# A fused attention, state-space and feed-forward layer: clamped decays, rows of the second weight pair loaded into spent space, and two steps in another order

## The reference

```
h    = rms_norm(x, pre_mix_w) * (1 + scale1) + shift1
q, k, v, xs, z, bm, cm, dt = split(h @ w_in)
attn = sliding window attention over blocks of 128 tokens (8 heads of 64)
ssm  = mamba2_mixer(xs, z, bm, cm, dt)           # 8 heads of 64, state 128, 2 groups
x    = x + gate1 * rms_norm(concat(attn, ssm) @ w_out, post_mix_w)
h    = rms_norm(x, pre_ffn_w) * (1 + scale2) + shift2
u    = causal_dwconv3(h @ w_up)                  # 1024 x 5632
x    = x + gate2 * rms_norm((gelu(u_gate) * u_val) @ w_down, post_ffn_w)
```

```
decay  = exp(segsum(dt * a))                     # zero above the diagonal
y_diag = einsum(cb * decay, xc)                  # cb = C B^T inside a block
y      = (y_diag + y_off + d_skip * xh) * silu(z)
y      = rms_norm over each of 2 groups of 256, times norm_w
```

## Time and profile before

| | |
|---|---|
| median of 3 runs | 1139.71 us (1139.21 to 1140.12) |
| the profiled execution | 1136.96 us, span 1135.0 us |
| TensorE busy | 1080.2 us, 95% of the span |
| VectorE busy | 867.8 us, 76% |
| ScalarE busy | 560.8 us, 49% |
| GpSimd busy | 250.1 us, 22% |
| largest groups of TensorE | L2099 407.1 us, L2496 359.5 us, L2429 393.5 us in its last stretch |
| chain that ended last | PE 80%, DVE 9%, ACT 4%, DMA 3%, issue 2% |

### The profile page before, as it was taken

The page is one execution under the profiler, slowest core; times in us unless marked ns, Lnnn a source line. Parts: engine busy times, 40 slices in busy tenths (PEclk is TensorE's granted clock), DMA queues, the critical chain, the costliest instruction groups (busy, mean ns, idle before and its releaser), DMA issues.

```text
span 1135.0 us, 14878 instructions
## 1 busy us (share of the span) xinstructions
PE 1080.2 (95%) x5096; PEld 868.2 (77%) x5096; DVE 867.8 (76%) x1121; ACT 560.8 (49%) x1012; POOL 250.1 (22%) x237
## 2 busy tenths in 40 slices
PE   4699999999989999997999999999999999999997
PEld 4578766766767888765888888888888888888885
DVE  5869676767558688778888888888888877777687
ACT  4812254556464655665544444444444545454453
POOL 2000011111224442215333333333333100000012
PEclk9899999999999999998999999999999999999999
DMA  9989401001234222224343434343433595632324
GB/s 355 307 265 319 131 23 34 20 20 37 58 113 146 76 94 74 74 73 150 132 163 112 153 124 153 124 145 132 145 132 111 193 388 206 213 102 93 102 85 167
DMA packets 117487, 157.40 MB, mean 139 GB/s; under 512 B 15292, under 2 KB 76221, under 8 KB 117437
## 3 DMA queue, kind: packets, MB, share of 16 engines
q1 hardware_dynamic: 117117, 155.69, 40.9%
q0 software_dynamic: 320, 1.06, 0.3%
HBM read 125.75 MB, written 30.98 MB: 138 GB/s over the span
## 4 chain that ended last, share of the span: by engine, by line
PE 80%; DVE 9%; ACT 4%; DMA 3%; issue 2%; POOL 1%; SPq 1%; DVEq 0%; POOLq 0%; ACTq 0%
PE ps L2429 35%; PE ps L2099 18%; PE ps L2496 18%; DVE big L1387 3%; DMA raw<-in_w_in_dram 2%; PE ps L2138 2%; PE ps L2164 1%; PE ps L2152 1%; DMA scratch<-in_rel_bias_dram 1%; DVE big L1765 1%; DVE w_lo L1428 1%; PE ps L2269 1%; PE ps L2055 1%; PE ps L2368 1%; PE ps L2197 1%
## 5 line engine op out<-in xcount | busy, mean ns | idle before, releaser
L2099 PE MATMUL ps<-a_hi,w_hi 128*128 128x512 f32 x416 | 142.7, 422 | 7.5 <-DVE a_lo L1447 3.8
L2099 PE MATMUL ps<-a_lo,w_hi 128*128 128x512 f32 x416 | 132.6, 397 | 0.0
L2099 PE MATMUL ps<-a_hi,w_lo 128*128 128x512 f32 x416 | 131.8, 395 | 0.0
L2496 PE MATMUL ps<-w_hi,a_hi 128*128 128x512 f32 x308 | 119.9, 389 | 0.2 <-DVE a_lo L1931 0.2
L2496 PE MATMUL ps<-w_lo,a_hi 128*128 128x512 f32 x308 | 119.8, 389 | 0.0
L2496 PE MATMUL ps<-w_hi,a_lo 128*128 128x512 f32 x308 | 119.8, 389 | 0.0
L1299 ACT ACTIVATE w_hi<-raw 128x512 fp32r<-128x512 f32 x77 | 48.7, 632 | 98.3 <-PE ps L2496 87.6
L2099 PEld LDWEIGHTS ps<-a_hi,w_hi 128*128 128x128 f32 x416 | 73.3, 192 | 29.6 <-issue 16.3
L1219 ACT ACTIVATE scratch<-ps 128x512 f32<-128x512 f32 x88 | 52.3, 594 | 87.0 <-PE ps L2429 87.0
L2099 PEld LDWEIGHTS ps<-a_hi,w_lo 128*128 128x128 f32 x416 | 79.2, 190 | 18.2
L2099 PEld LDWEIGHTS ps<-a_lo,w_hi 128*128 128x128 f32 x416 | 79.5, 191 | 17.8
(11 more groups left out here) (267 smaller groups left out, 2394.0 us busy)
## 6 DMA issues: line engine op xcount, KB each, us to landing
big<-in_w_ada_dram SPq DMA_DIRECT2D x20, 1024.0 KB, 8.7
raw<-in_w_up_dram SPq DMA_DIRECT2D x22, 512.0 KB, 5.1
big<-in_w_up_dram SPq DMA_DIRECT2D x22, 512.0 KB, 5.1
big<-in_w_down_dram SPq DMA_DIRECT2D x22, 512.0 KB, 6.4
down_weight_sums<-big SPq DMA_DIRECT2D x22, 512.0 KB, 3.4
raw<-down_weight_sums SPq DMA_DIRECT2D x44, 256.0 KB, 2.8
ffn_hidden<-big SPq DMA_DIRECT2D x21, 512.0 KB, 2.6
big<-ffn_hidden SPq DMA_DIRECT2D x21, 512.0 KB, 8.4
```

What stands on the lines that cost most here:

```text
L2099: mm = pe.matmul(out, lhs_of[a], rhs_of(b, j), start=first and p == 0, stop=last and p == 2)
L2496: mm = pe.matmul(bk, a[:, ts], rhs_op(s)[w], start=fresh and m == 0, stop=last and m == 2, skip_group_check=s // KH in (J6, J3, J7))
```

## The change

1. **Decays.** The sums are kept with their sign (`sums`, before `neg_sums`). ScalarE no longer waits for GpSimd but for the loaded row. For each group it does four Relu of 128x128, relu(sum - row), waits for them, and then one Exp of 128x512 with scale -1. For allowed pairs that is the same value as before; for the future it is at most 1, whatever the sum. VectorE makes `cbm`, C B with the future set to zero (128x256, out of PSUM, times the triangle `upper`), waits for it, and multiplies the decays by `cbm` in place of the PSUM bank. `no_future` and GpSimd's `decay_mask` are gone.
2. **Pair 1's rows.** At the last block SyncE waits until pair 0's first low part is made, pair 0's sums are made, the last scaling by norm_w is done and the a1 rows have landed. Then it loads a21 and, below, a11 and a12 of pair 1 into `raw_pair(0)`, and a22 into `normw`. The load behind the token sums is gone. GpSimd's sums of pair 1 read there and no longer wait for pair 0's sums to be split; pair 2's load waits for them (`s_us` at 4).
3. **Order.** In the last unit `z_transpose` stands a step ahead of `state_product`. ScalarE squares the gated rows of block 0 ahead of the third `w_out_hi`.
4. **Copy of pair 1.** ScalarE copies product 0 of pair 1 ahead of the high part of s34 and of pair 0's Gelu.

Context lines and renamed semaphores are left out of the diff.

```diff
--- before.py
+++ after.py
@@ -199,9 +199,9 @@
         bn = scratch[:, 3328:3584].rearrange("p (g n) -> p g n", g=2)
-        no_future = scratch[:, 3072:3200]
+        cbm = scratch[:, 3072:3328].rearrange("p (g n) -> p g n", g=2)
         sum_rows = scratch[0:NB * H, 3200:3328]
-        neg_sums = scratch[:, 3584:3648]
+        sums = scratch[:, 3584:3648]
@@ -316,8 +316,8 @@
-            if isinstance(p, int) and p == 1 and kind == "a1":
-                return scratch[:, 2048:3072]
+            if isinstance(p, int) and p == 1 and kind in ("a1", "a22"):
+                return scratch[:, 2048:3072] if kind == "a1" else normw[:, :]
             return {"a1": raw_pair(par)[:, 0:1024], "s12": weight_sum(p)[0], "a22": raw_pair(par)[:, 1536:2048],
@@ -615,6 +615,19 @@
                     load_decay(b + 3)
+                if b == NB - 1:
+                    sp.wait_ge(s_ul, weights_to(0, "a1"))
+                    sp.wait_ge(s_us, 2)
+                    sp.wait_ge(s_my, NB)
+                    sp.wait_ge(s_a1, 16)
+                    sp.dma_start(raw_pair(0)[:, T:T + 512].rearrange("p (k n) -> p k n", k=4),
+                                 w_up2[0:512, P + FF:2 * P + FF].rearrange("(k p) n -> p k n", p=P))\
+                        .then_inc(s_uw[1], 16)
+                    sp.dma_start(normw[:, :].rearrange("p (k n) -> p k n", k=4),
+                                 w_up2[512:1024, P + FF:2 * P + FF].rearrange("(k p) n -> p k n", p=P))\
+                        .then_inc(s_a1, 16)
+                    sp.dma_start(raw_pair(0)[:, 0:T].rearrange("p (k n) -> p k n", k=KT),
+                                 w_up2[:, P:2 * P].rearrange("(k p) n -> p k n", p=P)).then_inc(s_uw[1], 16)
                 if b == NB - 2:
@@ -625,10 +638,6 @@
                     load_xr(b + 2)
-            sp.wait_ge(s_tk, sums_to("t3", REST))
-            sp.wait_ge(s_bl, splits_to("b22", REST))
-            load_pair(1, 1)
-
             def load_sums(k):
@@ -647,7 +656,7 @@
                     sp.wait_ge(s_ul, weights_to(p, "a22"))
-                    sp.wait_ge(s_us, p * 2 + 2)
+                    sp.wait_ge(s_us, 4 if first else p * 2 + 2)
                     load_pair(p + 2, par)
@@ -774,14 +783,6 @@
-            def decay_mask(i):
-
-                pool.wait_ge(s_kl, 16 * (i + 1))
-                for g in range(GROUPS):
-                    dg = decay[:, g, :].rearrange("p (h l) -> p h l", h=4)
-                    pool.tensor_tensor(dg, dg, no_future.unsqueeze(1).to_broadcast([P, 4, P]),
-                                       ALU.add).then_inc(s_rd, 1)
-
             def normalise_probs(u):
@@ -792,27 +793,31 @@
                 normalise_probs(u)
-                if u == 30:
-                    pool.wait_ge(s_nf, 1)
-                    decay_mask(0)
...
-                raw_p, (one, two) = raw_pair(par), weight_sum(p)
+                raw_p = raw_pair(0 if isinstance(p, int) and p == 1 else par)
+                one, two = weight_sum(p)
                 a11, a12, a21, a22 = (raw_p[:, 512 * j:512 * j + 512] for j in range(4))
+                second = isinstance(p, int) and p == 1
+                if second:
+                    a22 = normw[:, :]
+                    pool.wait_ge(s_a1, 32)
                 pool.wait_ge(s_uw[par], (p // 2 + 1) * 32 if isinstance(p, int) else (p - par) * 16 + 32)
                 if not first:
-                    if isinstance(p, int):
+                    if second:
                         pool.wait_ge(s_mf, NB)
-                    pool.wait_ge(s_ul, weights_to(p - 1, "s12"))
+                    else:
+                        pool.wait_ge(s_ul, weights_to(p - 1, "s12"))
                 pool.tensor_tensor(one[:, 0:512], a21, a22, ALU.add).then_inc(s_uq, 1)
...
                 if not first:
-                    if isinstance(p, int):
+                    if second:
                         pool.wait_ge(s_x1[1], 16 * NB // 2)
                         pool.wait_ge(s_n2, NB)
-                    pool.wait_ge(s_ul, weights_to(p - 1, "s34"))
+                    else:
+                        pool.wait_ge(s_ul, weights_to(p - 1, "s34"))
                 pool.wait_ge(s_us, p * 2 + 1)
@@ -825,13 +830,9 @@
                     rstd(st[:, 40 + b:41 + b], st[:, 32 + b:33 + b], D, s_r2)
-                if 2 <= i < NB - 1:
-                    decay_mask(i + 1)
                 if i < NB:
...
                     rstd(st[:, 58:60], st[:, 56:58], SSM_W // GROUPS, s_gr)
-                if i < 2:
-                    decay_mask(i + 1)
                 if i == 0:
@@ -1075,12 +1076,13 @@
-                act.wait_ge(s_rd, 2 * i + g + 1)
+                act.wait_ge(s_kl, 16 * (i + 1))
                 for h in range(4):
...
                     n = i * H + 4 * g + h
-                    ins = act.activation(part, part, ACT.Exp, bias=neg_sums[:, n:n + 1])
-                ins.then_inc(s_E, 1)
+                    ins = act.activation(part, part, ACT.Relu, scale=-1.0, bias=sums[:, n:n + 1])
+                link(ins)
+                act.activation(decay[:, g, :], decay[:, g, :], ACT.Exp, scale=-1.0).then_inc(s_E, 1)
@@ -1144,9 +1146,10 @@
             last_tanh(0)
-            for k in range(3):
-                w_out_hi(k)
+            w_out_hi(0)
+            w_out_hi(1)
             gated_squares(0)
+            w_out_hi(2)
             w_out_hi(3)
@@ -1188,8 +1191,8 @@
-                if isinstance(p, int) and p == 1 and kind == "a1":
-                    act.wait_ge(s_a1, 16)
+                if isinstance(p, int) and p == 1 and kind in ("a1", "a22"):
+                    act.wait_ge(s_a1, 16 if kind == "a1" else 32)
                 elif kind in ("a1", "a22"):
@@ -1271,9 +1274,12 @@
                 copy_product(p - 1, 1 - par, 3, first=second)
+                if second:
+                    copy_product(p, par, 0)
                 weight_hi(p, par, "s34")
                 gelu(p - 1)
-                copy_product(p, par, 0)
+                if not second:
+                    copy_product(p, par, 0)
                 val_first_tap(p - 1, first=second)
@@ -1567,7 +1573,7 @@
                     .then_inc(s_dt2, 1)
-                dve.tensor_scalar(neg_sums, bank(5)[:, 256:320], -1.0, None, ALU.mult)
+                dve.tensor_copy(sums, bank(5)[:, 256:320])
                 dve.tensor_copy(sum_rows, bank(4)[0:NB * H, 256:256 + P]).then_inc(s_kr, 1)
@@ -1587,11 +1593,16 @@
                 dve.wait_ge(s_cb, i + 1)
+                if i == 0:
+                    dve.wait_ge(s_ks, 16)
+                dve.tensor_tensor(cbm, bank(7)[:, 0:2 * P].rearrange("p (g n) -> p g n", g=2),
+                                  upper.unsqueeze(1).to_broadcast([P, 2, P]), ALU.mult).then_inc(s_cbm, 1)
+                dve.wait_ge(s_cbm, i + 1)
                 for g in groups:
...
                     dg = decay[:, g, :].rearrange("p (h l) -> p h l", h=4)
-                    cb = bank(7)[:, g * P:(g + 1) * P].unsqueeze(1).to_broadcast([P, 4, P])
-                    dve.tensor_tensor(dg, dg, cb, ALU.mult).then_inc(s_W, 1)
+                    dve.tensor_tensor(dg, dg, cbm[:, g, :].unsqueeze(1).to_broadcast([P, 4, P]),
+                                      ALU.mult).then_inc(s_W, 1)
@@ -2285,8 +2295,8 @@
-                chunk_0 = {(0, 3): rows_and_b, (0, 6): cb_products, (1, 1): y_diag_products, (1, 2): state_product,
-                           (1, 3): z_transpose}
+                chunk_0 = {(0, 3): rows_and_b, (0, 6): cb_products, (1, 1): y_diag_products, (1, 2): z_transpose,
+                           (1, 3): state_product}
                 for hf in range(2):
```

7 lines of the change are left out of this document (3 added, 4 removed).

## The result

| | before | changed |
|---|---|---|
| median, 10 runs each | 1139.87 us (1137.11 to 1143.41) | 1133.43 us (1129.92 to 1138.78) |
| ratio | | 0.9939, 95% interval 0.9920 to 0.9959 |
| profiled execution (span) | 1136.96 us (1135.0) | 1132.14 us (1130.3) |

The change makes the kernel 6.4 us faster by the medians (0.6%), and the time lies in the range of the prediction.

What follows compares the result with a forecast made beforehand. From 523 us the kernel was taken as one run of TensorE work, so only earlier waits and half clock could go: blocks 2.0 plus pair 1 6.1 is 8.1 us, 1139.7 to 1131.6 us, range 1125.5 to 1135.5.

Steps and rivals of the forecast that it cites:

- blocks 3 to 7: Decays and masked C B of these blocks: the added ScalarE and VectorE work fits, 0 with 0.3 us either way.
- gained by the blocks: Blocks, from block 0's earlier rows on: 2.0 us; 3.0 if block 1's second product precedes GpSimd, 5.3 if the lock costs nothing.
- VectorE falls behind: Before the last token parts: four GpSimd sums of 1.25 us taking turns with VectorE put it 3.3 us behind.
- gained at that product: Pair 2's second product, 544.15 before: reached at 538.05, 6.1 us gained; 9.4 without the held 3.3 us.
- The lock: Block 1 and pair 1: VectorE and GpSimd take turns, whole operations, when both read two SBUF operands.
- Rival (a): Blocks and pair 1: the lock hardly costs, 5.3 and 9.4 us gained, 14.7 in all, 1125.0 us; chance 0.18.
- The clock: TensorE at half clock after idling: about 1.5 us more in block 1, partly hidden; none summed after pair 2's 2.65 us wait.
- rival (b): Clock falls before pair 2's second product; in block 1 GpSimd gets ahead, half clock paid fully: 5.1 us gained, 1134.6; chance 0.25.
- Part 4: ScalarE's list in pair 1: moving copy 0 ahead costs nothing, as it runs at 515 and is needed at 516.1.
- Rival (c): ScalarE's decays: Relu and Exp share no function table, reloads lose 24 us over six blocks, 1155 us; chance 0.03.
- Rival (d): Pair 1's early rows do nothing because a load or the sums come late; only 2.0 us gained, 1137.7; chance 0.04.
- the signs I named: Signs included no GpSimd in the chain from 380 to 460 us and GpSimd's first pair 1 sum near 487.

Runs made afterwards that it cites:

- e4_psum_product: Changed kernel with the decays multiplied by C B straight out of PSUM, not by the masked copy (output not the reference's); one execution, 1131.81 us.
- x3_s34_later: Changed kernel with GpSimd's last two sums of pair 1 waiting until the tokens' last low part is made; 1135.40 us, ratio to before 0.9950.
- e2_rows: Kernel before with only pair 1's rows loaded early into spent space, without the early copy of product 0; 1133.54 us, ratio 0.9945.
- x1_copy0: Changed kernel with ScalarE copying product 0 of every pair, not only pair 1, ahead of s34's high part and the Gelu; 1130.67 us, ratio to before 0.9913.
- e5_no_part4: Changed kernel with product 0 of pair 1 copied behind pair 0's Gelu again; 1134.97 us, ratio to before 0.9952.

## Why the prediction was right, and where it was off

The prediction counted in the times of the trace of before. The measured times are those of the changed kernel's trace less 2.13 us in the blocks (the late start), and less 0.23 us from block 7 on, where 1.9 of it had been won back.

| step | predicted | measured |
|---|---|---|
| row scaling of block 0, start and end | 334.1, 335.0 | 334.1, 335.0 |
| TensorE goes on after it | 338.4 | 338.3 |
| masked C B; a group of decays | 0.45; 1.95 us | 0.41; 1.85 us |
| y_diag of block 1, of block 2 | 346.7, 360.3 | 346.5, 360.0 |
| blocks 3 to 7 | 0, or 0.3 either way | 0.5 us lost |
| gained by the blocks | 2.0 us | 1.9 us |
| pair 1's loads issued; first sum | 479.1; 488.65 | 479.1; 488.7 |
| VectorE falls behind | 3.3 us | 2.6 us |
| TensorE's product with t1 | 498.2 | 497.5 |
| assembly that releases the first tap ends | 512.95 | 512.3 |
| TensorE at pair 2's product with t2 | 538.05 | 537.6 |
| gained at that product | 6.1 us | 6.6 us |
| half clock behind that wait | not in the sum | 1.7 us |
| sum, to the down products | 8.1 us | 6.7 us |

**The lock** was the right mechanism: e4_psum_product shows it in block 1 by the operand alone, x3_s34_later in pair 1 by moving the sums. Rival (a) did not come about: beside the four sums each of VectorE's operations took 1.0 to 1.1 us more. That the lock is what keeps the gain from (a)'s 14.7 us is not shown. Where it was taken out of block 1 the blocks gained 1.8 us in all and not 5.3, where it was taken off most of the token splits no idle time was gained, and both times other waits took its place. The prediction said that no row showed whether a one-operand VectorE operation is held too (and, a little further on, that VectorE's work there is all on two SBUF operands, which the normalise is not). It is held: the normalise of block 7 took 1.75 us beside GpSimd's first sum, 1.76 in e2_rows, and 0.75 in all seven other blocks. It moved the sum little, but TensorE waited 1.03 us for it. The Trainium skill ("SBUF — State Buffer", two separate sides) states that a VectorE operation in a 2-port mode takes the lock. The trace of the changed kernel agrees as far as it goes: it shows the hold, not the mode of the operation.

**The clock** is the term that was mis-sized. I let block 1 start at half clock and it did not. In x1_copy0 and x3_s34_later, which are the changed kernel up to block 7, it did, and block 7 came at 123.4 and 123.3: a gain of 1.0 and 1.1 us (and of nothing, 124.8, in e5_no_part4, where it stayed low for longer). So with the clock as I had put it the blocks would have given about half of my 2.0, because blocks 3 to 7 cost more than the nothing I had for them; that the blocks came out at 1.9 is in part luck. I let pair 2's product run at full clock after a wait that I put at 2.65 us. The wait was 2.26, and the clock fell to half 1 us later, 1.7 us lost: one half of rival (b) came true, the other half did not. At that product 1.9 + 6.6 = 8.5 us were gained, a little over my sum, and the half clock behind it is why 6.7 are left at the down products. The rows had a sign of it that I passed over: before the change the clock was already at half at 339.00, after a single wait of 2.2 us that ended at 338.3. In the split above half of the gain is not idle time at all: 3.2 us of 6.7 are idle time, 3.1 are half clock, and the latter differs from one execution to the next by more than that.

**Part 4** I had put down as costing nothing, and alone it gains nothing either: e5_no_part4 waits 2.5 us for the copy in pair 1, the changed kernel 2.3 in pair 2. I had not seen that the same edit in every pair takes 2.1 us of idle time and a half clock of 1.7 out of pair 2's stretch, though the wait it removes stood in the prediction.

**Rival (c)** is out: five table loads before and after, none among the decays, and the time is lower. **Rival (d)** is out: the loads were issued at 479.4 and the first sum ran at 488.91. Of the signs I named two were wrong. The first sum was to come near 487, where my own sum had 488.65 and it came at 488.7. And the chain of waits between 380 and 460 us still has GpSimd steps, roots at 390.88, 416.30 and 452.01. The mask's step at 386 us is gone, and with it nothing was gained in block 4, where TensorE waits 0.9 us and before 0.7.

What stays open is what makes the clock fall. With the same idle time of 3.0 us in block 1 it stayed in the changed kernel and fell in x1_copy0, x3_s34_later and e5_no_part4. No run was made to hold it up.

## What to carry to other kernels

When a transfer or a step is moved ahead of a busy stretch, price what it triggers there: here four small sums on an engine with nothing else to do put VectorE 2.6 us behind in its fullest stretch. Read a list of waits as one delay of the engine behind it, not as a sum: moving one copy moved the wait from pair 1 to pair 2 and no gain can be measured of it, moving it in every pair took it away. And split a gain into idle time and clock before reading a difference of some microseconds between two profiles.
